# The longest row tile of each head: turned by TensorE's transposes or by the DMA queue

## What is computed

```
q = rms_norm(c_q) @ w_uq ; k, v = rms_norm(c_kv) @ w_ukv      # 96 and 64 columns a head
q, k = rope_tail(rms_norm(q)), rope_tail(rms_norm(k))
for each block of 128 queries:
    s = (q_block @ k.T) * scale, masked to keys <= query
    p = softmax(s)
    o = p @ v
x = x + (o * silu(z)) @ w_out
```

## Time and profile before

| | before |
|---|---|
| runs | 963.10, 963.06, 962.77 us, median 963.06 |
| profiled execution | 963.16 us, its span 961.3 us, mean granted TensorE clock 0.998 |
| busy share of the span | PE 98%, PEld 70%, DVE 85%, ACT 60%, POOL 39% |
| DMA | 103.67 MB, transfers of q1 take 37.8% of the engines' time |

### The profile page before, as it was taken

One profiled execution on the slowest core, in us unless ns is written; L12 is line 12 of the kernel. 1 busy time (PEld: TensorE's weight loads), 2 busy tenths in 40 slices (PEclk: granted clock), 3 DMA queues, 4 the chain that ended last, 5 costly groups with the idle time before them and its releaser, 6 DMA issues.

```text
span 961.3 us, 16137 instructions
## 1 busy us (share of the span) xinstructions
PE 946.9 (98%) x5830; PEld 668.8 (70%) x5830; DVE 813.6 (85%) x1410; ACT 579.6 (60%) x1076; POOL 376.2 (39%) x425
## 2 busy tenths in 40 slices
PE   9999999999999999999999999999999999999998
PEld 7788544444688887644457999898778877887443
DVE  5798899899865579989787899988999999998763
ACT  7434544434434454454646888867999999998230
POOL 0002243222000002235412577857773589897220
PEclk9999999999999999999999999999999999999999
DMA  9320431111055422432023264566565766460231
GB/s 306 46 58 23 110 83 50 44 45 45 1 178 166 137 66 66 119 101 67 21 72 110 93 208 161 185 181 176 116 170 142 169 154 114 94 170 2 88 110 66
DMA packets 165343, 103.67 MB, mean 108 GB/s; under 512 B 75272, under 2 KB 149520, under 8 KB 165008
## 3 DMA queue, kind: packets, MB, share of 16 engines
q1 hardware_dynamic: 159216, 102.25, 37.8%
q10 hardware_dynamic: 6048, 0.39, 0.5%
HBM read 56.48 MB, written 29.36 MB: 89 GB/s over the span
## 4 chain that ended last, share of the span: by engine, by line
PE 79%; DVE 12%; POOL 3%; issue 3%; ACT 3%; POOLq 0%; DVEq 0%; ACTq 0%
PE banks L111 23%; PE banks L113 22%; PE banks L112 22%; PE banks L2732 5%; PE banks L2750 2%; PE banks L2751 1%; DVE front_lt L1223 1%; ACT front_set_b L723 1%; DVE heads_probs_big L2490 1%; DVE front_l L1223 1%; DVE front_w_row L1065 1%; ACT heads_probs_big L2352 1%; PE banks L2759 1%; DVE heads_pt_lo L2498 1%; DVE front_set_b L1082 1%
## 5 line engine op out<-in xcount | busy, mean ns | idle before, releaser
L2498 DVE TENSOR_TENSOR heads_pt_lo<-banks,heads_pt_hi 128x512 f16<-128x512 f32 (+2 forms) x192 | 102.1, 554 | 11.2 <-ACT heads_pt_hi L2361 7.0
L2361 ACT ACTIVATE heads_pt_hi<-banks 128x512 f16<-128x512 f32 (+2 forms) x192 | 88.4, 485 | 4.9 <-PE banks L2732 4.6
L2750 PE MATMUL banks<-heads_v,heads_pt_hi 128*128 128x128 f16 x576 | 74.5, 220 | 0.0
L2732 PE MATMUL banks<-ident,heads_probs_big 128*128 128x128 f32 x416 | 69.1, 279 | 1.4 <-ACT heads_probs_big L2352 1.3
L2751 PE MATMUL banks<-heads_v,heads_pt_lo 128*128 128x64 f16 x576 | 69.5, 193 | 0.0
L2490 DVE CUSTOM_DVE_ANT_0 heads_probs_big<-banks,heads_mask,score_scale 128x1024 f32<-128x1024 f32 (+1 forms) x64 | 68.5, 1071 | 0.9
L2352 ACT ACTIVATE heads_probs_big<-heads_probs_big,heads_neg_max 128x1024 f32<-128x1024 f32 (+1 forms) x64 | 63.4, 991 | 5.6 <-DVE heads_neg_max L2490 3.6
L111 PE MATMUL banks<-front_act_hi,front_w_hi 128*128 128x512 f32 x160 | 63.9, 399 | 0.3 <-DVE front_w_lo L943 0.3
L111 PE MATMUL banks<-heads_k_t,heads_q_t 96*128 96x512 f16 (+2 forms) x192 | 62.9, 327 | 0.9 <-DVE heads_neg_max L2490 0.9
L113 PE MATMUL banks<-front_act_hi,front_w_lo 128*128 128x512 f32 x160 | 62.4, 390 | 0.0
L112 PE MATMUL banks<-front_act_lo,front_w_hi 128*128 128x512 f32 x160 | 62.3, 389 | 0.0
(11 more groups left out here) (488 smaller groups left out, 3099.3 us busy)
## 6 DMA issues: line engine op xcount, KB each, us to landing
qk_scratch<-heads_y SPq DMA_DIRECT2D x22, 512.0 KB, 3.6
front_x<-in_x_t SPq DMA_DIRECT2D x16, 512.0 KB, 5.4
front_raw<-in_w_in_ab SPq DMA_DIRECT2D x14, 512.0 KB, 5.2
qk_scratch<-heads_last_y SPq DMA_DIRECT2D x10, 512.0 KB, 3.5
front_w<-in_w_out_ab SPq DMA_DIRECT2D x8, 512.0 KB, 3.8
x_scratch<-front_x SPq DMA_DIRECT2D x8, 512.0 KB, 4.0
v_scratch<-heads_v SPq DMA_DIRECT2D x32, 128.0 KB, 3.0
heads_v_st<-v_scratch SPq DMA_DIRECT2D x8, 512.0 KB, 5.1
```

The lines of the kernel that those rows point to most:

```text
L2361: nc.scalar.activation(pt_hi[:, q % PIECES, :width], t_ps[:, banks[("piece", n, k)] % 3, :width], ACT.Copy).then_inc(pt_high, 1)
L2498: nc.vector.tensor_tensor(pt_lo[:, q % PIECES, :width], t_ps[:, banks[("piece", n, k)] % 3, :width], pt_hi[:, q % PIECES, :width], ALU.sub ...
L2732: last = nc.tensor.transpose(t_ps[:, b, r * P:(r + 1) * P], probs(n, j * P, (j + 1) * P), ident[:])
L2750: nc.tensor.matmul(out, pt_hi[:, q % PIECES, blk], v2[e][:, j, :], start=(j == 0), stop=False)
```

## The change

From head 1 on, the first step of a head (tile 7, 1024 keys, step n = 8h; `by_queue`) is no longer transposed by PE, nor taken from accumulator banks. Instead ACT casts the whole 128x1024 row tile to a high part (`big_high`, one step ahead of step n), DVE subtracts it for the low part (`big_low`, in step n), and SP issues two DMA transposes of 128x1024 float16 within on-chip memory (`turn_big`, between `load_q` and the weights and values that it loads). PE multiplies the turned tile seven steps later (`big_product`, step 8h + 7, `BIG_BEHIND`). The ring of pieces has 5 buffers. `copy_out` of a head's first group moves from step 8h + 5 to step 8h + 8.

In all value products the high part of the probabilities is multiplied twice by 64 columns (high and low part of the values) in place of once by 128, all into the same 64 columns. So `copy_out` moves 256 columns, and the addition L2645 on POOL is gone.

`NORM_UNIT` is 26 instead of 24, `EXP_UNIT` 28 instead of 27. Buffers are placed elsewhere: the residual rows are loaded when all scores are made, instead of straight after the last K and Q, two of the four sums of weights lie elsewhere, and the last ones wait for the last `big_product`. POOL's helpers wait on one chained semaphore instead of several.

```diff
         self.w_row, self.w_size, self.w_scale, self.unscale = [field(self.OUT_PAIRS) for _ in range(4)]
...
         self.stage = [at(f"stage{n}", [P, BANK], F32, w_place + 2 * FORMS * half + n * half) for n in range(4)]
-        res_at = self.res_at = (ring_at, ring_at + 3 * tile, spare + 6 * 1024, spare + 6 * 1024 + tile)
+        res_at = (ring_at, ring_at + 3 * tile, ring_at + tile, ring_at + 2 * tile)
+        self.v_at = spare + 10 * 1024
+        self.big = [at(name, [P, NK, P], F16, place) for name, place in (
+            ("big", spare + 10 * 1024), ("big_lo", w_place + GROUP_W * 4 + 10 * 1024))]
+        self.big_t = [at(name, [P, NK, P], F16, place) for name, place in (
+            ("big_t", spare + 12 * 1024), ("big_t_lo", spare))]
+        self.big_high, self.big_low, self.big_done, self.big_in = sem("big_high"), sem("big_low"), sem("big_done"), sem("big_in")
...
             sp.wait_ge(self.stored[n], self.res_base[n] + 32 * (m // self.PLACES_OF_ROWS))
-        elif m >= self.PLAIN:
-            sp.wait_ge(self.plain_done, self.split_base + self.PLAIN)
...
             dve.wait_ge(self.w_in[m + n], 32)
-        if q == 0:
-            dve.wait_ge(self.joint.s_added, 4 * ALL_PAIRS + 4)
+        if q < 2:
+            dve.wait_ge(self.joint.s_added, 4 * (ALL_PAIRS + q) + 4)
...
-    AHEAD, BEHIND, TURN_LAG, PIECES = 2, 2, 5, 6
+    AHEAD, BEHIND, TURN_LAG, PIECES, BIG_BEHIND = 2, 2, 5, 5, 7
...
-    o_raw = at("o_raw", [P, 2, 4, 2 * VH], F32, o_at)
+    o_raw = at("o_raw", [P, 2, 4, VH], F32, o_at)
...
+    def by_queue(n):
+        return n > 0 and n % NT == 0
+    def parts(n):
+        return [] if by_queue(n) else pieces(tile_of(n)[1])
+    piece_base = [0]
+    for n in range(N):
+        piece_base.append(piece_base[-1] + len(parts(n)))
...
-        h, p = divmod(n, NT)
-        return PER_HEAD * h + sum(len(pieces(ORDER[x])) for x in range(p)) + k
+        return piece_base[n] + k
...
-    NORMS, NORM_UNIT, EXP_UNIT = (4, 7, 8, 9, 11, 15, 16, 17, 19, 23), 24, 27
+    NORMS, NORM_UNIT, EXP_UNIT = (4, 7, 8, 9, 11, 15, 16, 17, 19, 23), 26, 28
...
             sp.dma_start(v_st[:], by_tile(v_d)[:, :, h * VH:(h + 2) * VH]).then_inc(v_in, 16)
+        def turn_big(h):
+            for part, made in enumerate((out.big_high, out.big_low)):
+                sp.wait_ge(made, h)
+                if h > 1:
+                    sp.wait_ge(out.big_done, h - 1)
+                sp.dma_start_transpose(out.big_t[part][:], out.big[part][:].rearrange("p b k -> p (b k)")
+                                       ).then_inc(out.big_in, 16)
...
             load_q(h)
+            turn_big(h - 1)
...
                 store_qk(LATE_LOW + h - 2)
+        turn_big(HEADS - 1)
+        sp.wait_ge(s_ready, N)
...
+        def big_high(n):
+            h = n // NT
+            if h == 1:
+                for e in range(VSLOTS):
+                    act.wait_ge(v_stored[e], 16 * len(range(e, UNITS, VSLOTS)))
+            act.wait_ge(exp_done, n + 1)
+            act.wait_ge(out.big_in, 32 * (h - 1))
+            nc.scalar.activation(out.big[0][:].rearrange("p b k -> p (b k)"), probs(n, 0, S), ACT.Copy).then_inc(out.big_high, 1)
         def copy_out(g):
+            if g % 2 == 0 and g:
+                act.wait_ge(out.big_done, g // 2)
...
             if g >= 2:
-                act.wait_ge(o_summed, g - 1)
-            nc.scalar.activation(o_raw[:, g % 2], o_ps[:, g % 2], ACT.Copy,
+                act.wait_ge(o_scaled, g - 1)
+            nc.scalar.activation(o_raw[:, g % 2], o_ps[:, g % 2, :, :VH], ACT.Copy,
...
             if n < N:
-                for k in range(len(pieces(tile_of(n)[1]))):
+                for k in range(len(parts(n))):
...
                 exponentials(n + AHEAD)
+            if by_queue(n + 1) and n + 1 < N:
+                big_high(n + 1)
             if n >= BEHIND and (n - BEHIND) % 4 == 3:
-                copy_out((n - BEHIND) // 4)
+                if (n - BEHIND) // 4 % 2 or n < NT:
+                    copy_out((n - BEHIND) // 4)
+            if n % NT == 0 and n > NT:
+                copy_out(2 * (n // NT) - 2)
...
                     out.gate_high(act, NK - 2, c)
-        act.wait_ge(pv_done, PER_HEAD * HEADS)
+        act.wait_ge(pv_done, piece_base[N])
...
             dve.wait_ge(s_ready, n + 1)
-            if n >= 4:
-                dve.wait_ge(pt_ready, piece_no(n - 4, len(pieces(tile_of(n - 4)[1])) - 1) + 1)
+            if n >= 4 and by_queue(n - 4):
+                dve.wait_ge(out.big_low, (n - 4) // NT)
+            elif n >= 4:
+                dve.wait_ge(pt_ready, piece_base[n - 3])
...
                                     pt_hi[:, q % PIECES, :width], ALU.subtract).then_inc(pt_low, 1)
+        def big_low(n):
+            h = n // NT
+            dve.wait_ge(out.big_high, h)
+            dve.wait_ge(out.big_in, 32 * (h - 1))
+            nc.vector.tensor_tensor(out.big[1][:].rearrange("p b k -> p (b k)"), probs(n, 0, S),
+                                    out.big[0][:].rearrange("p b k -> p (b k)"), ALU.subtract).then_inc(out.big_low, 1)
...
             if n < N:
-                for k in range(len(pieces(tile_of(n)[1]))):
+                for k in range(len(parts(n))):
                     low(n, k)
+                if by_queue(n):
+                    big_low(n)
...
             pair, e = h // 2, h % 2
-            raw = o_raw[:, g % 2]
             pool.wait_ge(o_copied, g + 1)
-            nc.gpsimd.tensor_tensor(o_sum[:, g % 2], raw[:, :, :VH], raw[:, :, VH:], ALU.add).then_inc(o_summed, 1)
-            pool.wait_ge(o_summed, g + 1)
...
             nc.gpsimd.tensor_tensor(
-                pair_tiles(pair, g, e), o_sum[:, g % 2].rearrange("p (a b) d -> p a b d", a=2),
+                pair_tiles(pair, g, e), o_raw[:, g % 2].rearrange("p (a b) d -> p a b d", a=2),
...
             pool.wait_ge(joint.form_low, FORMS * (ALL_PAIRS + q))
+            pool.wait_ge(out.big_done, HEADS - 1)
...
             q = piece_no(n, k)
-            if n % NT == 0 and k == 0:
+            first = 1 if by_queue(n - 1) else 0
+            if n % NT == first and k == 0:
                 pe.wait_ge(v_low, h + 1)
-            if n % 4 == 0 and k == 0:
+            if n % 4 == (first if n % NT < 2 else 0) and k == 0:
...
             pe.wait_ge(pt_low, q + 1)
-            out = o_ps[:, g % 2, o_slot(i), :]
+            o_part = o_ps[:, g % 2, o_slot(i), :VH]
...
                 blk = slice(r * P, (r + 1) * P)
-                nc.tensor.matmul(out, pt_hi[:, q % PIECES, blk], v2[e][:, j, :], start=(j == 0), stop=False)
-                last = nc.tensor.matmul(out[:, :VH], pt_lo[:, q % PIECES, blk], v2[e][:, j, :VH],
+                nc.tensor.matmul(o_part, pt_hi[:, q % PIECES, blk], v2[e][:, j, :VH], start=(j == 0), stop=False)
+                nc.tensor.matmul(o_part, pt_hi[:, q % PIECES, blk], v2[e][:, j, VH:], start=False, stop=False)
+                last = nc.tensor.matmul(o_part, pt_lo[:, q % PIECES, blk], v2[e][:, j, :VH],
...
             last.then_inc(pv_done, 1)
+        def big_product(n):
+            h = n // NT
+            e, o_part = h % 2, o_ps[:, n // 4 % 2, o_slot(NT - 1), :VH]
+            pe.wait_ge(out.big_in, 32 * h)
+            for j in range(NT):
+                nc.tensor.matmul(o_part, out.big_t[0][:, j], v2[e][:, j, :VH], start=(j == 0), stop=False)
+                nc.tensor.matmul(o_part, out.big_t[0][:, j], v2[e][:, j, VH:], start=False, stop=False)
+                last = nc.tensor.matmul(o_part, out.big_t[1][:, j], v2[e][:, j, :VH], start=False, stop=(j == NT - 1))
+            last.then_inc(out.big_done, 1)
...
             old = n - BEHIND
-            new_pieces = len(pieces(tile_of(n)[1])) if n < N else 0
-            old_pieces = len(pieces(tile_of(old)[1])) if 0 <= old < N else 0
+            new_pieces = len(parts(n)) if n < N else 0
+            old_pieces = len(parts(old)) if 0 <= old < N else 0
+            big = n - BIG_BEHIND
...
                     transposes(n, k)
+                if k == 0 and by_queue(big) and big < N:
+                    big_product(big)
...
             for pair in range(PAIRS):
```

More of the change, by code:

```diff
@@ L1708, in __init__ @@
         self.w_row, self.w_size, self.w_scale, self.unscale = [field(self.OUT_PAIRS) for _ in range(4)]
-        sum_places = (joint.rstd_at, ring_at + tile, ring_at + 4 * tile)
-        self.sums = [[at(f"sums{q}_{n}", block, F32, place + (n if q or n < 3 else 2) * half)[:]
-                      for n in range(4) if q or n != 2]
-                     for q, place in enumerate(sum_places)]
-        self.sums[0].insert(2, self.quarter_of(0, 1, 0))
+        sum_places = [(joint.rstd_at, joint.rstd_at + half, None, spare + 6 * 1024),
+                      (spare + 8 * 1024, spare + 10 * 1024, None, spare + 12 * 1024),
+                      [ring_at + 4 * tile + n * half for n in range(4)]]
+        self.sums = [[self.quarter_of(q, 1, 0) if place is None else at(f"sums{q}_{n}", block, F32, place)[:]
```

(31 more changed lines are left out.)

27 lines of the change are left out of this document (11 added, 16 removed).

## The result

The changed kernel takes 969.65 us (median of 4 runs, 969.25 to 970.44) against 963.08 us (4 runs of the kernel before, 962.77 to 963.39): ratio 1.0068, 95% interval 1.0056 to 1.0080. It is 6.6 us slower; 956.5 was forecast, with a range up to 966.

The account below looks back on a forecast made before the run. PE was taken as the bound, with DVE, ACT and POOL close behind and DVE limiting after the change. Terms -5.7 - 2.2 + 1.5 - 0.3 = -6.7 us gave 956.5 us; 8 times in 10 between 949 and 966.

Parts of the forecast that it names:

- The pace: Attention, 15 heads: 13.2 us a head instead of 13.58, set by DVE; -5.7 us (-12.9 to +1.8).
- my lower bound: DVE's 1024-column subtraction for the long tile: 1.21 us undisturbed; 1.5 us was taken, up to 1.90.
- DVE takes the gain: Rival, attention: large subtraction 1.9 us beside POOL and idle time stays, 13.55 us a head; 961.7 us; chance 0.19.
- The turned tile is late: Rival, step 8h + 7: PE waits at big_product for the low half's DMA; 981 or 967 us; chance 0.11.
- The work removed was cover: Rival, attention: PE's eight transposes only filled time it would have waited anyway; 962.2 us; chance 0.03.
- Narrow products cost a weight load: Rival, value products: 0.0425 us for each narrow matmul, PE 14.2 us a head; 971.8 us; chance 0.07.
- The norms' product: Before the attention: two units later, PE's stand goes, gain limited by DVE's idle time; -2.2 us (0 to -3.9).
- the 3.9 us offered: PE's time around the norms' product: 2.18 us of standing still plus 1.7 us lost to the lower clock.
- Values and turns: Late pairs: values land later, so PE may wait for POOL at the turn, 0.5 us in three pairs; +1.5 us.
- The end: Last pair's turn: its 0.29 us wait for POOL goes with the removed addition; -0.3 us (0 to -0.7).

Follow-up runs that it names:

- x_noprod: Changed kernel with the turned tile multiplied in only two of its eight blocks, 18 of 24 matmuls left out: 964.42 us, ratio 1.0012.
- b8: Changed kernel with the turned tile multiplied eight steps on instead of seven: 963.94 us, ratio 1.0010.
- the kernel without queue: Changed kernel with every row tile transposed on PE, copies in their old steps, ring of six pieces; later norms and narrow products stay: 961.84 us, ratio 0.9985.

## Why the prediction was wrong

**The pace, -5.7 us: measured +5.2 up to 856 us, the failed step.** Its sum for DVE was right (12.96 us a head, 12.99 forecast); the failure is "PE's work is then 13.58 - 0.88 + 0.02 = 12.72 us a head" used as if the step didn't matter, and the pace read off the larger total, with 0.2 us idle. DVE's idle time was 14.06 - 12.96 = 1.1 us a head, and its share fell, which the prediction had named as a sign of its failing. Totals are right only if an engine can save time in one step and spend it in another. Here the 0.88 us go out of one step, where DVE and ACT had as much to do as before, and the products come back in another, where PE had no room: 5.2 us by x_noprod and 5.7 by b8. When only transposes go, six of the eight, a head takes 13.17 us, so the premise held in the main for that half (0.46 of 0.66 us). The subtraction takes 1.22 us undisturbed, as my lower bound, not 1.5. With the product in its step it hides in a wait in the quiet heads; at eight steps, cutting it gives 4.7 us, mostly where it meets GpSimd.

**"DVE takes the gain"** named the right engine for what is left at eight steps, but not the loss: it ended at no change. **"The turned tile is late"** had the right sign and the wrong mechanism: it lands 3.1 us after issue, no wait of PE for the queue is seen in the changed kernel, and without transfers the kernel isn't faster. **"The work removed was cover"** (0.03) had the nearest mechanism: the transposes were cover for about half of their time (4.7 to 5.4 of 9.9 us came back). What it lacked is the price of putting other work elsewhere. **"Narrow products cost a weight load"** is refuted: 0.029 us apart, and 1.1 us won. Its 971.8 us was the rival's time nearest to the measured one, but by luck. (Its limit is also wrong: by the sum of the earlier trace rows, three narrow matmuls eat up the 0.88 us at 0.0365 us each, not 0.033.)

**The norms' product, -2.2: measured 0.** PE's stand and the low clock around it went (PE busy 50.00 of 600 to 650 us, clock 1.00), and the first maximum came 0.88 us earlier (658.37). But both halves of the 3.9 us offered came back at 660 to 670 us: a stand of 1.8 us for ACT's squares and a mean clock of 0.83. The bound should have been followed one wait further. **Values and turns, +1.5**: GpSimd waited up to 5.0 us for values, but no turn waited visibly in the full pairs; nothing. **The end, -0.3**: not separated, hidden in the +1.2.

**What stays open.** Why b8 isn't faster than the kernel without queue: the subtraction with its collisions (4.7 us; two of the subtractions take 2.0 to 2.1 us and three 1.5 to 1.7 for 1.22) is shown to matter, the copies (0.9 us at five steps) are not clear of the noise, but no run adds them up to the 2.1 us between the two. The K issues only place it: the kernel with eight steps is 0.9 us later at 701 us, gains 0.8 us in the five quiet heads, is level in the next six, and loses 1.4 us behind the last issue. The step table by which I chose five steps was wrong and I did not replace it; the success of eight steps was expected from the same table, so its sign is shown and its arithmetic isn't.

## What to carry to other kernels

Where three engines are above 0.9 busy and each may run only a step or two ahead, a sum over a period can give a gain that isn't there, or the wrong sign: make the sum for the step that loses work and for the step that gets it. Work that returns later should return into the step that lost it: here that was worth 5.7 us, though it only made up for the loss. And when a wait is removed, follow the chain to the next operand: here the next stand, of nearly the same length and with the same low clock, took back all of it.

## What the runs showed of the hardware

A transposing DMA from on-chip memory to on-chip memory, 128x1024 in f16, is issued in 1.23 us and lands after 3.1 us; K's, of twice the bytes and from DRAM, lands after 5.1 us. 64-column f16 matmuls, each with other weights, start 0.029 us apart. A VectorE subtraction of two on-chip operands that begins inside a GpSimd instruction of that kind takes 2.61 instead of 1.22 us, and a GpSimd cast that begins inside it takes 2.03 instead of 1.04 us. Fewer transfers can so cost time: 28 less made this kernel 5 us slower. The granted clock fell to a mean of 0.83 over 10 us around a stand of PE of 2.18 us in one kernel and of 1.82 us in others; in two profiled executions with the same stand of 1.82 us (five steps, and the queue's tile in heads 1 to 7) it stayed at 1.00, and the K issues before and behind that stretch are 20.3 us apart there, instead of 21.7 in the changed kernel.
